# Memory attention of a hybrid decoder step: prompt heads, sample keys and output products in another order

## What is computed

```python
# 1. mixer: conv branch and latent attention side by side, one output projection
u = u_val * sigmoid(u_gate)
conv_out = silu(layernorm(causal_conv31(u), ln_g, ln_b))         # 512 channels
out = concat([conv_out, attn_out], -1) @ w_out                    # attn_out: 8 heads x 64
x = x + out
# 2. memory attention, 4 heads x 128, 256 memory tokens
q = (rmsnorm(x) @ w_mq).reshape(b, t, 4, 128)
p = softmax(einsum('bthd,bmhd->bhtm', q, mem_k) * 128 ** -0.5)
x = x + einsum('bhtm,bmhd->bthd', p, mem_v).reshape(b, t, 512) @ w_mo
# 3. top-4-of-32 experts, width 1024, clamped SwiGLU
x = x + moe(rmsnorm(x))
y = rmsnorm(x)
```

## Time and profile before

| what | value |
|---|---|
| median of 3 runs | 1382.13 us (lowest 1382.11) |
| the profiled execution, whole | 1381.29 us |
| its span, first to last instruction | 1379.5 us |
| around the span | 1.8 us |
| mean granted TensorE clock | 0.975 |
| TensorE matmul busy | 1299.7 us (94%) |
| VectorE / ScalarE busy | 450.0 us (33%) / 217.8 us (16%) |
| DMA | 463.37 MB, mean 336 GB/s |

### The profile page before, as it was taken

How to read it: one execution, slowest core, us unless ns; L and a number is a source line. 1 busy time by engine, 2 the same in 40 slices (tenths; PEclk the granted TensorE clock), 3 DMA queues, 4 the chain that set the end, 5 groups by cost and what they waited for, 6 DMA issues and landing times.

```text
span 1379.5 us, 15552 instructions
## 1 busy us (share of the span) xinstructions
PE 1299.7 (94%) x6088; PEld 527.1 (38%) x6088; DVE 450.0 (33%) x1124; ACT 217.8 (16%) x442; POOL 15.5 (1%) x20
## 2 busy tenths in 40 slices
PE   7999897987779999999999999999999999999996
PEld 3665654455343333333333333333333333333332
DVE  1167687223252223222222223222232222222233
ACT  3014333213230001101001000100101100011002
POOL 0100020000000000000000000000000000000000
PEclk9999998999969999999999999999999999999999
DMA  9701131490358999999999999999999999999993
GB/s 325 283 12 41 35 138 62 175 374 0 150 247 353 429 425 428 427 429 427 427 429 428 427 427 430 427 428 427 430 427 427 428 429 427 427 430 427 428 426 125
DMA packets 44249, 463.37 MB, mean 336 GB/s; under 512 B 5190, under 2 KB 6150, under 8 KB 17844
## 3 DMA queue, kind: packets, MB, share of 16 engines
q1 hardware_dynamic: 42684, 453.54, 78.7%
q0 software_dynamic: 1536, 9.44, 1.8%
HBM read 460.04 MB, written 3.28 MB: 336 GB/s over the span
## 4 chain that ended last, share of the span: by engine, by line
PE 77%; DMA 13%; DVE 7%; ACT 2%; issue 1%; SPq 0%; ACTq 0%; DVEq 0%
PE psum L864 41%; DMA ring<-in_w_up 12%; PE psum L839 6%; PE psum L324 5%; PE psum L880 4%; PE psum L403 2%; DVE ring L1498 2%; PE psum L857 2%; PE psum L363 2%; PE psum L619 2%; PE psum L693 1%; PE psum L381 1%; PE psum L884 1%; PE psum L590 1%; PE psum L791 1%
## 5 line engine op out<-in xcount | busy, mean ns | idle before, releaser
L864 PE MATMUL psum<-ring,work 128*64 128x512 f32 x3168 | 700.6, 595 | 7.4 <-DMA ring<-in_w_up 7.3
L864 PEld LDWEIGHTS psum<-ring,work 128*64 128x64 f32 x3168 | 220.9, 137 | 477.4 <-issue 445.5
L1863 DVE TENSOR_SCALAR work<-psum 128x512 f32<-128x512 f32 x32 | 22.1, 692 | 377.2 <-PE psum L864 377.2
L839 PE MATMUL psum<-H,work 128*64 128x512 f32 (+1 forms) x408 | 101.0, 614 | 1.4 <-DVE work L1754 1.4
L1872 DVE TENSOR_SCALAR work<-psum 128x512 f32<-128x512 f32 x32 | 22.1, 692 | 170.3 <-PE psum L864 170.3
L1827 DVE TENSOR_TENSOR X<-X,psum 128x512 f32<-128x512 f32 x68 | 46.6, 686 | 90.0 <-PE psum L880 89.9
L1498 DVE SCALAR_TENSOR_TENSOR ring<-ring,cwT 128x256 f32<-128x256 f32 x240 | 72.5, 376 | 0.1
L324 PE MATMUL psum<-C,work 128*128 128x128 f32 (+5 forms) x371 | 57.2, 288 | 9.8 <-DMA work<-in_small_rows 6.9
L1363 ACT COPY work<-psum 128x512 f32<-128x512 f32 x32 | 18.8, 587 | 292.9 <-PE psum L839 292.9
L1370 ACT COPY work<-psum 64x512 f32<-64x512 f32 x32 | 18.5, 578 | 286.6 <-PE psum L864 286.6
L324 PEld LDWEIGHTS psum<-C,work 128*128 128x128 f32 (+5 forms) x371 | 48.8, 187 | 34.6 <-issue 22.4
(11 more groups left out here) (291 smaller groups left out, 928.2 us busy)
## 6 DMA issues: line engine op xcount, KB each, us to landing
ring<-in_w_gate SPq DMA_DIRECT2D x66, 2048.0 KB, 24.2
ring<-in_w_up SPq DMA_DIRECT2D x66, 2048.0 KB, 26.1
ring<-in_w_down SPq DMA_DIRECT2D x66, 2048.0 KB, 28.1
ring<-in_w_in SPq DMA_DIRECT2D x1, 4096.0 KB, 28.9
ring<-in_w_out SPq DMA_DIRECT2D x2, 2048.0 KB, 8.3
ring<-in_cache_mem_k SPq DMA_DIRECT2D x8, 512.0 KB, 13.3
ring<-in_cache_mem_v SPq DMA_DIRECT2D x8, 512.0 KB, 15.3
ring<-in_w_in SPq DMA_DIRECT2D x1, 2688.0 KB, 23.8
```

The lines of the kernel that those rows point to most:

```text
L839: last = mm(psum[64 * nh:64 * nh + 64, 2, :], Ph[0:ROWS[tt], tt, :], xn[0:ROWS[tt], tt, 512 * nh:512 * nh + 512], start=tt == 0, stop=tt == 2)
L864: last = mm(psum[64 * nh:64 * nh + 64, bank, :], src[:, j, 64 * half:64 * half + 64], w[:, half, j, 512 * nh:512 * nh + 512], start=first ...
L1863: v.tensor_scalar(gm, psum[:, 0, :], LIMIT, None, ALU.min).then_inc(s.g_clip, 1)
```

## The change

TensorE, last pair:

```diff
                 else:
-                    ln_mean()
                     pe.wait_ge(s.load_wout, 16)
                     emptied(pe, V, ("pa_o", 3))
                     first = [S.open(pe, ("out", 0, nh)) for nh in range(2)]
                     for nh in range(2):
                         out_part(first[nh], 0, nh, (4, 5, 6, 7))
+                sa_turn(pair)
+                if pair == 3:
+                    ln_mean()
+                sa_values(pair)
+                if pair == 3:
                     ln_var()
-                sa_turn(pair)
-                sa_values(pair)
...
-            pe.wait_ge(s.load_wout, 32)
+            pe.wait_ge(s.load_wout2, 16)
             pe.wait_ge(s.ln_out, 4)
             for nh in range(2):
-                out_part(first[nh], 0, nh, (0, 1, 2, 3)).then_inc(s.full_s, 1)
+                out_part(first[nh], 0, nh, (0, 1))
+            pe.wait_ge(s.load_wout3, 16)
+            for nh in range(2):
+                out_part(first[nh], 0, nh, (2, 3)).then_inc(s.full_s, 1)
```

SP, the load of the second half of `w_out` in two pieces of 1 MB:

```diff
+            sp.wait_ge(s.conv_done, 1)
+            dma(w_out[:, 4:6, :], rows_of(a["w_out"][0])[:, 0:2, :]).then_inc(s.load_wout2, 16)
             sp.wait_ge(s.ln_out, 4)
-            dma(w_out[:, 4:8, :], rows_of(a["w_out"][0])[:, 0:4, :]).then_inc(s.load_wout, 16)
+            dma(w_out[:, 6:8, :], rows_of(a["w_out"][0])[:, 2:4, :]).then_inc(s.load_wout3, 16)
```

TensorE, memory attention. The loops are gone; the order is written out (`queries(h)` is the old body of the query loop, `mo_part(tt, nh)` the old body of the `mo` loop):

```diff
+            flip_tile("h2T", 1, 1, by_block)
+            ms_keys(0)
+            flip_tile("h2T", 1, 2, by_block)
+            emptied(pe, V, ("h2T", 2, 0))
+            pe.wait_ge(s.load_wmq, 16)
+            queries(0)
+            queries(1)
+            ma_scores(0)
+            queries(2)
+            ma_scores(1)
+            ma_turn(0)
+            queries(3)
+            ma_scores(2)
+            ma_turn(1)
+            ms_keys(1)
+            ma_values(0)
+            ms_scores(0)
+            ma_scores(3)
+            ms_keys(2)
+            ma_values(1)
+            ma_turn(2)
+            ms_scores(1)
+            ms_keys(3)
+            ms_scores(2)
+            ma_values(2)
+            ms_keys(4)
+            ms_scores(3)
+            ma_turn(3)
+            ms_keys(5)
+            ms_scores(4)
+            ma_values(3)
+            ms_keys(6)
+            ms_scores(5)
+            ms_keys(7)
+            ms_scores(6)
+            pe.wait_ge(s.load_wmo, 16)
+            emptied(pe, V, ("ma_o", 3))
+            mo_part(0, 0)
+            ms_scores(7)
+            mo_part(0, 1)
             pe.wait_ge(s.mem_prob, MH + 1)
             ps = A.open(pe, "ss_t")
...
             last.then_inc(s.full_a, 1)
+            mo_part(1, 0)
             emptied(pe, A, "ss_t")
...
                 last.then_inc(lane.full, 1)
+            mo_part(1, 1)
             for bg in range(2):
                 lane = (V, A)[bg]
                 emptied(pe, lane, ("ss_o", bg))
...
-            pe.wait_ge(s.load_wmo, 16)
+            flip_tile("h3T", 2, 0, by_stride)
             for bg in range(2):
                 emptied(pe, (V, A)[bg], ("ss_f", bg))
-            for tt in range(2):
-                for nh in range(2):
-                    ps = V.open(pe, ("mo", tt, nh))
...
-            flip_tile("h3T", 2, 0, by_stride)
             halves = [V.open(pe, ("mo", 2, nh)) for nh in range(2)]
```

ScalarE and VectorE take their parts in the same written-out order. Around the samples' softmax:

```diff
 # ScalarE
             mem_exp(psum[:, 6, :], MH, ss_p)
             move("ss_t", ...)
+            f(small[:, 17:18], eps[:, :], ACT.Sqrt)
+            emptied(act, V, ("mo", 0, 1))
+            norm_root(0)
             move(("ss_o", 1), lambda ps: [(so[1], ps)])
             move(("ss_f", 1), own_head(1))
-            f(small[:, 17:18], eps[:, :], ACT.Sqrt)
-            for tt in range(3):
+            for tt in range(1, 3):
 # VectorE
             mem_max(psum[:, 6, :], MH)
+            add_tile(V, s.free_v, "mo", 0, (0,))
             mem_prob(MH, ss_p)
+            add_tile(V, s.free_v, "mo", 0, (1,))
+            add_tile(V, s.free_v, "mo", 1, (0,))
+            norm(2, 0)
             give(v.tensor_copy(so[0], V.take(dve, ("ss_o", 0))))
+            add_tile(V, s.free_v, "mo", 1, (1,))
```

More of the change, by code:

```diff
@@ L682, in _ @@
                         last.then_inc(s.full_v, 1)
[L685 to L694, removed]
             def ma_scores(h):
@@ L742, in ms_scores, with queries, mo_part @@
                 last.then_inc(s.st_full, 1)
[L744 to L757, removed]
+            def queries(h):
+                lane = (A, V)[h % 2]
+                ps = lane.open(pe, ("qm", h))
+                for k in range(KD):
+                    last = mm(ps[:, 0:T], wmq[:, k, 128 * h:128 * h + 128], hT[:, k, :], start=k == 0, stop=k == KD - 1)
+                last.then_inc(lane.full, 1)
+            def mo_part(tt, nh):
+                ps = V.open(pe, ("mo", tt, nh))
+                for h in range(MH):
+                    last = mm(ps, oT[:, h, tok(tt)], wmo[:, h, 512 * nh:512 * nh + 512], start=h == 0, stop=h == MH - 1)
+                last.then_inc(s.full_v, 1)
+            flip_tile("h2T", 1, 1, by_block)
[38 more added lines that the diff above has]
+            mo_part(0, 1)
             pe.wait_ge(s.mem_prob, MH + 1)
@@ L1268, in _ @@
                     pa_move(2 * pair + 2)
+                sa_move_turned(pair)
+                if pair < 3:
+                    sa_move(2 * pair + 3)
                 else:
@@ L1274, in _ @@
                     f(lnstd, ps[:, 0:T], ACT.Sqrt, bias=eps[:, :], scale=1.0 / CH).then_inc(s.free_a, 1)
[L1275 to L1282, removed]
                 sa_move_out(pair)
@@ L1285, in _ @@
                     pa_move(2 * pair + 3)
+            for ct in range(4):
+                act.wait_ge(s.ln_scaled, 1)
+                f(mixT[:, ct, :], CA[:, ct, :], ACT.Silu, bias=vecT[:, V_LB + ct:V_LB + ct + 1],
+                  scale=vecT[:, V_LG + ct:V_LG + ct + 1]).then_inc(s.ln_out, 1)
             f(small[:, 17:18], eps[:, :], ACT.Sqrt)
@@ L1316, in mem_keys, with mem_query, mem_turned, mem_head @@
                 move(("mkcT", b, 1), lambda ps: [(mkT[b % 2][:, 512:1024], ps)])
[L1318 to L1325, removed]
+            def mem_query(h):
+                move(("qm", h), lambda ps: [(qmT[:, h, :], ps[:, 0:T])])
+            def mem_turned(h):
+                move(("ma_t", h), lambda ps: [(mpt[h % 2], ps)])
+            def mem_head(h):
+                mem_exp(A.take(act, ("ma_s", h)), h, mp[h % 2])
+            mem_keys(0)
+            mem_query(0)
+            mem_head(0)
+            mem_query(2)
+            mem_head(1)
+            mem_turned(0)
+            mem_head(2)
+            mem_turned(1)
+            mem_keys(1)
+            mem_head(3)
+            mem_keys(2)
+            mem_turned(2)
+            mem_keys(3)
+            mem_keys(4)
+            mem_turned(3)
+            mem_keys(5)
+            mem_keys(6)
+            mem_keys(7)
             mem_exp(psum[:, 6, :], MH, ss_p)
@@ L1646, in _ @@
             norm(1, 2)
[L1647 to L1661, removed]
             def mem_max(ps, h):
@@ L1679, in mem_keys @@
                 give(v.tensor_copy(mkT[b % 2][:, 0:512], ps))
[L1681 to L1690, removed]
@@ L1691, in _, with mem_query, mem_head, mem_out @@
-            for b in range(MH, DEC_B):
-                mem_keys(b)
+            def mem_query(h):
+                ps = V.take(dve, ("qm", h))
+                give(v.tensor_copy(qmT[:, h, :], ps[:, 0:T]))
+            def mem_head(h):
+                produced(dve, A, ("ma_s", h))
+                mem_max(A.bank(A.index["ma_s", h]), h)
+            def mem_out(h):
+                ps = V.take(dve, ("ma_o", h))
+                give(v.tensor_copy(oT[:, h, 0:SEQ], ps[:, 0:SEQ]))
+            mem_keys(0)
@@ new lines, in _ @@
+            take_tile("h2T", gains, 2)
+            for bg in range(2):
+                st(v.memset(qz[bg], 0.0))
+            mem_query(1)
+            mem_head(0)
+            mem_prob(0, mp[0])
+            mem_head(1)
+            mem_prob(1, mp[1])
+            mem_query(3)
+            mem_head(2)
+            emptied(dve, V, ("qm", MH - 1))
+            emptied(dve, A, ("qm", MH - 2))
+            st.wait()
+            for bg in range(2):
+                padded = qz[bg].rearrange("p (h x) -> p h x", h=MH)
+                for b4 in range(4):
+                    c0 = SEQ + 32 * bg + 8 * b4
+                    last = v.tensor_copy(padded[:, :, 40 * b4:40 * b4 + 8], qmT[:, :, c0:c0 + 8])
@@ L1693, in _ @@
+            last.then_inc(s.qz_ready, 1)
+            mem_keys(1)
+            mem_out(0)
+            mem_prob(2, mp[0])
+            mem_head(3)
+            mem_keys(2)
+            mem_out(1)
+            mem_prob(3, mp[1])
+            mem_keys(3)
+            mem_out(2)
+            mem_keys(4)
+            mem_keys(5)
+            mem_out(3)
+            mem_keys(6)
+            mem_keys(7)
+            v.memset(part[:, T:384], 0.0)
             dve.wait_ge(s.st_full, DEC_B)
             mem_max(psum[:, 6, :], MH)
```

(1 more changed line is left out.)

27 lines of the change are left out of this document (8 added, 19 removed).

## The result

The median went from 1382.12 to 1345.26 us (the four runs of the changed kernel from 1339.61 to 1349.06): a ratio of 0.9733, 95% interval 0.9702 to 0.9765. I had predicted 1350.7 us and a range from 1345.5. One of the four executions of the kernel before took 1721.95 us, in place of about 1382; nothing here rests on it. The profiled execution took 1347.15 us, span 1345.3. It is compared here with the profiled one of before (span 1379.5), so 34.2 us are to be placed.

What follows compares the result with a forecast made beforehand. The expert stage was taken as bound by its weight stream, whose first refill waits on the work before. Savings of 7.3 + 24.1 = 31.4 us from 1381.29 gave 1349.9, plus 0.8 for the median: 1350.7 us, range 1345.5 to 1360.

Steps and rivals of the forecast that it cites:

- What bounds the kernel: Expert stage bound by its weight stream; each microsecond saved before the first refill at 416.54 us moves the end.
- Part 1: Last pair, layer norm and output product: attention half of tile 0's product fills the conv wait; 7.3 us saved.
- a clock that falls at the start: First L619 product in the last pair: clock falls to 0.50, half of a 3.5 us recovery lost, 1.7 us.
- Part 2: Memory attention to tile 2's product: 85.11 us becomes 61.0, including 0.6 for small stalls; 24.1 saved, bounds 17 and 26.
- the kept one: Wait between tile 0's flips and tile 2's product, 0.5 us, the only one expected to stay in memory attention.
- the slow clock at the queries: Start of memory attention: first of three slow stretches, 0.35 x 6.96 us lost, all three counted as gained.
- Part 3: Router, ranks and first products behind memory attention: distances kept, weight loads still covered, no cost.
- the clock that stays low: Queries and L774 lose 4.8 us again, L619 0.7 more; 25.9 saved, 1356.2 us; chance 0.12.
- New stalls: Written-out order: a late softmax holds PE, five chains stay half open; 22 us saved, 1360 us; chance 0.08.
- a low clock throughout: Memory attention at clock 0.50: 121 us against 85, 36 lost, 7 gained, 1410 us; chance 0.02.
- the gain would not reach the end: Stream set by something other than the first refill: 1382 us or a little less; chance 0.03.
- theory B: From the experiments, not the prediction: spread comes from DMA (page gathers, weight stream); no chance given.

Runs made afterwards that it cites:

- part1_only: Kernel before with only the last pair's new order and w_out's load in two pieces, memory attention as before: 1369.18 us, ratio 0.9913.
- nosplit: Changed kernel with the second half of w_out loaded in one 2 MB piece after ln_out: 1351.24 us, ratio 0.9777.
- 37.3 at the second: Median of the changed kernel run once more, unedited: 1344.74 us, ratio 0.9736.
- products_back: Changed kernel with all four of the prompt's output products back behind the samples' chain: 1355.3 us, ratio 0.9813.
- warm_routing: Changed kernel with unread products in front of five of PE's waits between tile 2's product and the experts: 1339.22 us, ratio 0.9695.
- part 2 alone: Kernel before with only the new memory attention: 1350.21 us, ratio 0.9775.

## Why the prediction was right and where it was wrong

**What bounds the kernel: right.** From the first refill to the end it took 962.2 to 963.9 us in all twelve profiles, whatever came before. Each microsecond ahead of the refill reached the end.

**Part 1: right in its chain, mis-sized in the clock.** The column sums moved behind the product, the wait is gone, `ln_out` came at 255.4 and the last 1 MB landed 5.7 us behind its issue, in time (PE needed it at about 261.4, 0.3 us later, by an estimate from 250.92 and half of 20.87). I charged 1.7 us for a clock that falls at the start. It fell in part1_only and nosplit (8.68 and 8.78 us for the 16 instructions) and didn't in the other six profiles with this order (7.10 or 7.11). So the term was 0 or some 1.6, by execution, and I had put one value in the sum: 9.4 measured against 7.3. This is the largest term of the sum that was mis-sized. The rest, 0.4, is the small tile's flips at full clock ahead of the queries.

**Part 2: right.** 25.0 saved against 24.1. The 0.6 us for small stalls wasn't needed: no wait is left but the kept one. Head 0's chain took 4.4 us (297.22 to 301.59 in the timeline) and its flips started at 302.23, so the margin was 0.6 us where I had 0.9. The sum held a mistake that hid: I had counted the slow clock at the queries as gained, since `ms_keys(0)` fills part of the idle time and gaps of 1.5 us had left the clock at 1.00 elsewhere. The length of a gap doesn't decide it: behind gaps of 1.3 and 0.8 us the clock fell in six of the seven profiles with this order and nothing in the gaps, and stayed up in nosplit. In after it fell, and the first two heads took 10.57 us instead of 8.9. The stretch before that shows it at 0.60:

```profile
285.10:289.20 4.10, 3.42 (x7) 2.25 (x8) 1.60 (x3) 0.00 (x0) 0.00 (x0) 0.60 1.02 432
```

That cost 1.7 us. It didn't show because I had counted the work too high: without the 1.7 and the kept wait of 0.39 the stretch is 58.0 us, where I had 59.9 and 0.6 for stalls. (The upper bound of 26 us for this part doesn't come out of its terms either: 24.1 and the 0.6 for stalls make 24.7.) Products that follow each other without a wait overlap their drains, which the busy time of before, cut up by waits, held many times over; that explanation is argued, not tested.

The Trainium skill, "ScalarE: Activation LUTs", "What ACT_TABLE_LOAD costs", puts a table switch at about 2.66 us with its drain. The trace of after doesn't agree: it has the load at 298.23 for 1.28 us and the exponential at 299.52. By an estimate from the page's figure PE would have waited 0.8 us at head 0; it waited 0.

**Part 3: the step that failed.** "Router, ranks and the first products keep their distances ... No cost." They keep their work and not their time. The same instructions took from 30.5 to 37.2 us, because PE idles between small operations there, the clock falls 6.5 to 11.3 us into the stretch, and stays low for 10.2 to 27.3 us. With unread products in the idle times the clock stays at 1.00 and the stretch takes 27.9. The trace of before had it, at a mean clock of 0.66:

```profile
381.38:416.54 35.16, 28.04 (x131) 13.57 (x133) 17.24 (x64) 11.11 (x21) 0.00 (x0) 0.66 0.53 219
```

I had read three other slow-clock stretches as costs that can go, and took this one as fixed. In the profiled execution it went against me, 2 us longer than before. At the median of after it was, by an estimate, some 34 us (1344.7, the median of its nine runs, less 1.8 around the span, 962.8 behind the refill and 346.1 ahead of the stretch), 1 us less than before.

**The sum.** 31.4 predicted; 36.9 at the first median, 37.3 at the second. Of the difference 2.1 lie in part 1, 0.9 in part 2 and about 1 in part 3. The rest, some 1.5, lies ahead of the change, where executions differ by more than that (1.1 between the two profiles compared). The two parts alone, 34.4 us as measured, would give 1347.7, inside the range. What took the median out of it, by 0.2 us, lies outside the parts: my range was built from bounds inside them only and had no term for the routing stretch or the start. That the median fell just below the range and not just inside it is chance.

**The rivals.** Of the clock that stays low, the half at the queries came true and cost 1.7; L774 and L619 ran at full clock. New stalls didn't come; nor did a low clock throughout (0.97). That the gain would not reach the end is refuted by every profile.

## What to carry to other kernels

In an in-order engine a wait costs twice when the clock falls in it, and a product with no reader near it is worth more as a cover than its own length: 3.5 us of product hid 4.6 here. Before you call a stretch unchanged, look at its granted clock; if it is below 1.00, its length isn't a property of its instructions, and your range needs a term for it. And compare two or three profiles of the kernel before, since two runs 0.02 us apart said nothing about its spread of 7.

## What I had not expected of the hardware

- Up to the end of the prompt's values all these kernels issue the same instructions on PE, and they took from 229.62 us (products_back) to 234.08 (warm_routing). Three places differ: the first weights let L363 start at 12.5 to 13.6 us, its 64 instructions take 27.73 to 30.45 us, and the first pair's values (L590) 3.67 or 5.2 to 5.3 us. The third is the clock, at 0.50 in the long case. The first two are at least in part DMA: PE waited 3.7 us for `in_w_mk` in products_back and 5.9 in warm_routing, with the clock at 1.00 in both. So theory B holds for a part of the spread.
- Filling PE's idle time with work that nobody reads made the routing stretch 2.6 to 9.3 us shorter. The Trainium skill says of the clock, in "TensorE: Matmul & The Clock Gate", Part 1, that activity lifts the slow default and that the ramp is "run-variable". These traces agree, and show how much that can be in one kernel: 6.65 us between two executions of the same program.
- Why the kernel before had 35.1 us in both of its profiles, part 1 and part 2 alone 31.5 and 31.2, and the changed one 37.2 and 30.5, isn't settled. That it is the clock is shown by the two kernels that keep it up; why it comes back when it does was not tried.
